# Third block's activations moved from the dense up stage to fetched rows, low parts taken on TensorE, gates spread in plain fp32

## The chip, the cores and the metric

The kernel runs on one core of a Trainium2 chip. The metric is the device time of one execution in microseconds (us), median over runs. The engines are PE (TensorE, matmuls, with its weight loads as PEld), DVE (VectorE), ACT (ScalarE), POOL (GpSimd) and SP (SyncE, which issues most DMAs). They run their own instruction streams and meet at semaphores.

## The reference

One layer of a streaming encoder over 512 tokens of width 1024 (8 chunks of 128): a mixer (stick-breaking attention and a gated short convolution), then a product-key retrieval over 16384 single-neuron experts, then a norm. The change touches the retrieval:

```
q = (x_blk @ w_q).reshape(n, PEER_HEADS, 2, PEER_HALF)        # 8 heads, two halves
s = jnp.einsum('nhpc,hpkc->nhpk', q, keys32)                  # 128 scores for each half
top_s, top_i = lax.top_k(s, PEER_TOPK)                        # first ranking: 16 of 128
cand_s = top_s[:, :, 0, :, None] + top_s[:, :, 1, None, :]    # 16 x 16 sums
best_s, best_c = lax.top_k(cand_s.reshape(...), PEER_TOPK)    # second ranking: 16 of 256
expert_idx = ...; gate = jax.nn.softmax(best_s, axis=-1)
act = jax.nn.gelu(jnp.einsum('nhkd,nd->nhk', expert_u[expert_idx], x_blk))
out = jnp.einsum('nhk,nhkd->nd', gate * act, expert_v[expert_idx])
```

So each token uses 8 x 16 = 128 experts, a row of 1024 values of `expert_u` and one of `expert_v` for each. All is fp32.

## The kernel before

Tokens are four blocks of 128. The first 487 us (the mix stage) do the mixer, the queries and the scores; it hands over the normed input `xn` transposed and split in a high part (`xnTh`, in the rounded format fp32r) and a low part (`xnTl`).

The fourth block (`SPARSE`) is done by rows: for each of its 128 slots, POOL issues an indirect DMA (`fetch`) that brings one row of 4 KB for each of 128 tokens into a ring of buffers, and DVE (`row`) forms the dot product with `x3` (rows of `expert_u`), or adds the weighted row to `acc` (rows of `expert_v`).

The first three blocks (`DB` = 3, 384 tokens) are done densely, as if every token used every expert.

**Up stage**, 128 steps, one for each group of 128 experts. In step n PE transposes the next group's `expert_u` tile into PSUM (`transposes`, 8 matmuls against the identity), ACT copies it to `uh`, rounding it (`high`), DVE subtracts to get `ul` (`low`), and PE forms activations for 384 tokens with 24 matmuls (`products`: 8 chunks times `uh`·`xnTh`, `uh`·`xnTl`, `ul`·`xnTh`). ACT applies the gelu and stores the result through its own DMA queue (`gelu`: the store of step n-2 must have landed, since `hb` has two buffers). SP loads the `u_raw` tiles four ahead.

Between the steps the gates are spread onto the 128 x 128 grid of experts. DVE ranks, finds the keys (`keys`) and builds one-hot matrices of 8 tokens (`one_hots`); ACT and POOL multiply them by the gate's high and low part (`hi`, `lo`); PE forms for 4 tokens at a time the product of one-hot and gate-one-hot, both parts side by side, 256 columns (`spread`); ACT copies them (`evac`), POOL adds the parts into `grid` (`gather`), SP stores the grid (`send`). Tables of step numbers (`HOT`, `SPREAD`, `KEYED`, `rows_of`) say in which step each engine does what; each engine works its own list in program order, and only semaphores hold it back. There is one spread in each of 96 steps.

**Down stage**, 32 turns z: 4 tiles of `expert_v` with activation times gate as weights. SP loads activations (`dh`), gates (`dg`) and values (`v_raw`); DVE multiplies (`weights`), ACT rounds (`rows_hi`, `weights_hi`), DVE subtracts (`rows_lo`, `weights_lo`) and PE does 72 matmuls of 512 columns (`down`). DVE works rows of the fourth block after the subtractions of each turn, the first 103 of its 256 rows already in the up stage. The ring has 5 buffers for the first 128 rows and 7 after. At the end the sums are added and normed.

## Time and profile before

| | us |
|---|---|
| median of 3 runs | 1715.44 (1713.63 to 1715.93) |
| span of the profiled execution | 1714.0 |
| mix stage (0 to 487) | 487 |
| up stage (487 to 1185) | 698 |
| down stage (1185 to 1707) | 522 |
| last adds and norm | 7 |

The span lies inside the range of the runs, 1.4 us under their median. The stages are cut at PE's first product, at its first matmul of the down stage and at its last matmul. PE is busy nearly all the time and runs at its full clock.

### The profile page before, as it was taken

To read this page: it belongs to the slowest core of one execution; us is meant where nothing else is said; L and a number is where in the kernel's file an instruction comes from. 1 tells how busy PE (TensorE), PEld (TensorE's weight loads), DVE (VectorE), ACT (ScalarE), POOL (GpSimd) and SP (SyncE) were. 2 spreads that over 40 slices of the span, in tenths; PEclk is the share of its full clock that TensorE was granted. 3 is DMA by queue.
4 is the path that set the end of the run, shared out by engine and by line. 5 is a ranking of instruction groups with operands and counts; after the bars stand their busy time and mean duration, and the time that the engine had idled before them with its cause. 6 is when DMAs were issued, how large, how long until landed. Compare 5 with 4: busy or idle time off the path is not lost.

```text
span 1714.0 us, 24432 instructions
## 1 busy us (share of the span) xinstructions
PE 1690.2 (99%) x9073; PEld 1510.9 (88%) x9073; DVE 1327.7 (77%) x1864; ACT 782.1 (46%) x1132; POOL 785.5 (46%) x494
## 2 busy tenths in 40 slices
PE   8999999999999999999999999999999999999998
PEld 6887788878899999999999999999888888888886
DVE  3666622265898999989999889976888888888887
ACT  6444433344333666746666566654323323323223
POOL 4333243333702555655555777771463443433430
PEclk9999999999999999999999999999999999999999
DMA  5222233322336666686667988888999999999992
GB/s 160 75 73 86 62 87 98 91 85 82 111 112 219 219 221 228 232 312 205 227 234 243 357 287 295 295 307 306 394 387 396 393 382 383 389 374 390 383 388 89
DMA packets 212443, 413.88 MB, mean 241 GB/s; under 512 B 11520, under 2 KB 150816, under 8 KB 207008
## 3 DMA queue, kind: packets, MB, share of 16 engines
q1 hardware_dynamic: 156880, 253.51, 42.4%
q0 software_dynamic: 36864, 134.23, 21.7%
q10 hardware_dynamic: 18640, 25.45, 4.2%
q8 instruction: 24, 0.39, 0.1%
q14 instruction: 35, 0.29, 0.1%
HBM read 360.73 MB, written 52.43 MB: 241 GB/s over the span
## 4 chain that ended last, share of the span: by engine, by line
PE 91%; DVE 5%; ACT 2%; issue 1%; DMA 0%; ACTq 0%; SPq 0%; DVEq 0%
PE psum L1375 30%; PE psum L1316 29%; PE psum L284 20%; PE psum L1306 6%; PE psum L1343 2%; PE psum L358 1%; PE psum L512 1%; DVE ul L1571 1%; DVE hot L1634 1%; PE psum L372 1%; PE psum L345 1%; DVE ring L1646 1%; DVE hot L1636 0%; DMA acc<-in_x 0%; ACT xTh L546 0%
## 5 line engine op out<-in xcount | busy, mean ns | idle before, releaser
L1316 PE MATMUL psum<-xnTh,uh 128*128 128x384 f32 x1024 | 353.8, 345 | 3.3 <-DVE ul L1571 3.1
L1316 PE MATMUL psum<-xnTl,uh 128*128 128x384 f32 x1024 | 343.4, 335 | 0.0
L1316 PE MATMUL psum<-xnTh,ul 128*128 128x384 f32 x1024 | 343.4, 335 | 0.0
L236 POOL TENSOR_TENSOR wl<-raw,wh 128x1024 fp32r<-128x1024 f32 x72 | 176.4, 2455 | 280.0 <-ACT wh L586 279.5
L1375 PE MATMUL psum<-vh,dwh 128*128 128x512 f32 x768 | 298.8, 389 | 0.2 <-DVE dwl L1664 0.2
L1375 PE MATMUL psum<-vh,dwl 128*128 128x512 f32 x768 | 298.8, 389 | 0.0
L1375 PE MATMUL psum<-vl,dwh 128*128 128x512 f32 x768 | 298.8, 389 | 0.0
L1530 POOL DMA_INDIRECT ring<-in_expert_v,index x128 | 170.9, 1335 | 248.9 <-DVE acc L1651 207.5
L1448 ACT ACTIVATE vh<-v_raw 128x4096 fp32r<-128x4096 f32 x31 | 112.7, 3635 | 339.0 <-PE psum L1375 338.5
L1530 POOL DMA_INDIRECT ring<-in_expert_u,index x128 | 176.1, 1375 | 165.0 <-DVE ring L1646 92.3
L1646 DVE SCALAR_TENSOR_TENSOR ring<-ring,x 128x1024 f32<-128x1024 f32 x128 | 209.7, 1659 | 6.4 <-DMA ring<-in_expert_u,index 5.1
L1549 POOL TENSOR_TENSOR grid<-parts 128x512 f32<-128x512 f32 x96 | 150.0, 1563 | 122.6 <-ACT parts L1441 98.6
L1316 PEld LDWEIGHTS psum<-xnTh,uh 128*128 128x128 f32 x1024 | 192.5, 188 | 6.5 <-DVE ul L1571 6.3
L1316 PEld LDWEIGHTS psum<-xnTl,uh 128*128 128x128 f32 x1024 | 192.7, 188 | 0.0
L1316 PEld LDWEIGHTS psum<-xnTh,ul 128*128 128x128 f32 x1024 | 192.3, 188 | 0.0
L1655 DVE TENSOR_TENSOR vl<-v_raw,vh 128x4096 fp32r<-128x4096 f32 x31 | 137.2, 4425 | 60.8 <-ACT vh L1448 60.8
L1571 DVE TENSOR_TENSOR ul<-psum,uh 128x1024 fp32r<-128x1024 f32 x128 | 155.6, 1216 | 29.6 <-ACT uh L1400 29.6
L1651 DVE SCALAR_TENSOR_TENSOR acc<-ring,weight,acc 128x1024 f32<-128x1024 f32 x128 | 164.3, 1283 | 10.7
L1375 PEld LDWEIGHTS psum<-vh,dwh 128*128 128x128 f32 x768 | 144.2, 188 | 30.3 <-issue 0.5
L1375 PEld LDWEIGHTS psum<-vh,dwl 128*128 128x128 f32 x768 | 144.2, 188 | 30.0
L1375 PEld LDWEIGHTS psum<-vl,dwh 128*128 128x128 f32 x768 | 144.2, 188 | 29.8
L284 PE MATMUL psum<-xTh,wh 128*128 128x512 f32 x424 | 168.4, 397 | 0.4 <-DVE xTl L973 0.4
(230 smaller groups left out, 2925.0 us busy)
## 6 DMA issues: line engine op xcount, KB each, us to landing
u_raw<-in_expert_u SPq DMA_DIRECT2D x128, 512.0 KB, 3.9
v_raw<-in_expert_v SPq DMA_DIRECT2D x30, 2048.0 KB, 14.6
expert_act<-hb ACTq DMA_DIRECT2D x128, 192.0 KB
expert_gate<-grid SPq DMA_DIRECT2D x12, 2048.0 KB, 7.2
dh<-expert_act SPq DMA_DIRECT2D x32, 768.0 KB, 5.6
dg<-expert_gate SPq DMA_DIRECT2D x32, 768.0 KB
raw<-in_w_in SPq DMA_DIRECT2D x40, 512.0 KB, 3.8
raw<-in_w_q SPq DMA_DIRECT2D x16, 512.0 KB, 3.9
```

What stands on the lines that cost most here:

```text
L236: nc.gpsimd.tensor_tensor(wl[slot][:], raw[slot][:], wh[slot][:].bitcast(F), ALU.subtract).then_inc(w_lo[slot], 1)
L284: done = nc.tensor.matmul(out, w[slot][:, at, :], x[:, i, :], start=(first and n == 0), stop=(last and n == 2))
L1306: last = nc.tensor.transpose(utp[s][:, c * P:(c + 1) * P], raw[n % 4][:, c * P:(c + 1) * P], ident[:])
L1316: last = nc.tensor.matmul(zb[s][:, 0:DT], w[s][:, c, :], x[:, c, 0:DT], start=(c == 0 and i == 0), stop=(c == C - 1 and i == 2))
L1375: last = nc.tensor.matmul(sums[k], w[s][:, j, b * P:(b + 1) * P], v[s][:, j, half * T:(half + 1) * T], start=(first and j == 0 and n == 0) ...
L1448: nc.scalar.activation(vh[s][:], v_raw[s][:], ACT.Copy).then_inc(v_hi[s], 1)
L1530: nc.gpsimd.indirect_dma_start(out=ring[k][:], out_offset=None, in_=tables[x // SLOTS], in_offset=bass.IndirectOffsetOnAxis(ap=index[:, x ...
L1549: nc.gpsimd.tensor_tensor(grid[:, :, n0:n0 + 4].rearrange("p k n -> p n k"), parts[x % 2][:, :, 0, :], parts[x % 2][:, :, 1, :], ALU.add). ...
L1571: nc.vector.tensor_tensor(ul[s][:].rearrange("p c f -> p (c f)"), utp[s], uh[s][:].rearrange("p c f -> p (c f)").bitcast(F), ALU.subtract) ...
L1646: nc.vector.scalar_tensor_tensor(at, at, 1.0, x3, ALU.mult, ALU.mult, accum_out=dots[:, k:k + 1]).then_inc(S["row_used"], 1)
L1651: nc.vector.scalar_tensor_tensor(acc3, at, weight[:, k:k + 1], acc3, ALU.mult, ALU.add).then_inc(S["row_used"], 1)
L1655: nc.vector.tensor_tensor(vl[s][:], v_raw[s][:], vh[s][:].bitcast(F), ALU.subtract).then_inc(v_lo[s], 1)
```

## The change

Four things are changed, and the tables of steps are written anew.

1. The third block (`MIXED`) gets its activations by fetched rows, as the fourth does: 128 more rows of `expert_u` (`x2`, `dots2`, `index2`), whose gelu then is multiplied into its gates (`gate_rows`). The dense up stage works on 256 tokens (`UT`). The down stage still has 384 columns of weights; for the third block they are the gates alone, copied from `dg`. In all 384 rows are fetched instead of 256: 203 of them are worked in the up stage, 53 by turn 9, 128 (of `expert_v`) in the 22 turns after. The ring has 7 buffers up to row 195, 5 for rows 196 to 215, then 7 others (0 to 4, 7, 8). POOL does nothing but fetch in the up stage.
2. The low part of `expert_u` tiles: PE adds minus the high part to the transposed tile in PSUM (`take_high`, 2 matmuls of 512 columns against `minus`, the negated identity, between the two halves of `products`), and ACT copies the rest as `ul` (`low`). DVE no longer takes part.
3. Gates are spread in plain fp32, 128 columns for a token: DVE builds the gate-one-hot itself with 8 small operations (`one_hots`), and ACT copies PSUM straight into one of two `grid` buffers, where neighbours lie 128 bytes apart. The first block has one spread a step (steps 40 to 71), the second and third have two (80 to 95, 104 to 119).
4. The second ranking looks at 112 of 256 sums (4 x 16 and 12 x 4), and six small operations (`cells`) turn a place among them into its two numbers.

```diff
-AHEAD = 8
...
+SEND = {spread_step(8 * q + 7) + 1: q for q in range(BATCHES // 4)}
...
+FIRST_RANKS = (11, 14, 18, 22)
+RANK_STEPS = {0: tuple(range(8, 28)), 1: (*range(37, 54, 2), 63, 65, 67)}
+KEYED = {MIXED: (4, 5, 6, 7), 0: (28, 29, 31, 33), SPARSE: (55, 57, 59, 61), 1: (69, 70, 71, 73)}
...
+GATED_IN = {5: (MIXED, SPARSE), 30: (0,), 70: (1,)}
+EXPS = {6: (MIXED, SPARSE), 31: (0,), 71: (1,)}
+GATED_OUT = {8: SPARSE, 9: MIXED, 34: 0, 74: 1}
...
+ROW_GELU, ROW_GATE = 96, 98
...
+IN_UP = 211
+LAST_DOT = 9
...
+    if n < 8 or n > 125 or n in KEY_STEP:
         return 0
...
+    if n < 28:
+        return 1 if n % 4 == 1 else 2
+    if n < 63:
+        return 1 if n % 6 == 0 else 2
+    if n < 72:
         return 0
...
+    return 3 if n % 4 == 0 else 2
...
-    return IN_UP + 5 * z if z <= 5 else SLOTS + (z - 5) * SLOTS // (2 * ROUNDS - 6)
+    if z <= LAST_DOT:
+        return FIRST_DOTS + (2 * SLOTS - FIRST_DOTS) * z // LAST_DOT
+    return min(3 * SLOTS, 2 * SLOTS + (z - LAST_DOT) * SLOTS // (2 * ROUNDS - 1 - LAST_DOT))
...
+WIDE_RING, EARLY, LATE = 196, 7, 216
...
-    for x in range(2 * SLOTS):
-        k = x % RING if x < SLOTS else (x - SLOTS) % RING_D
+    for x in range(3 * SLOTS):
+        k = x % EARLY if x < WIDE_RING else x % 5 if x < LATE else (0, 1, 2, 3, 4, 7, 8)[x % 7]
...
-    hot = [m.put(f"hot{i}", kb, [P, 8, 3, KEYS], R) for i, kb in enumerate((152, 32))]
...
+    hot = [m.put(f"hot{i}", kb, [P, 8, 2, KEYS]) for i, kb in enumerate((152, 32))]
...
-    ring = [m.put(f"ring{i}", kb, [P, D]) for i, kb in enumerate((187.75, 191.75, 195.75, 199.75, 203.75, 140, 180))]
+    ring = [m.put(f"ring{i}", kb, [P, D]) for i, kb in enumerate(
+        (187.75, 191.75, 195.75, 199.75, 203.75, 160, 164, 140, 180))]
...
             for c in range(C):
-                last = nc.tensor.transpose(utp[s][:, c * P:(c + 1) * P], raw[n % 4][:, c * P:(c + 1) * P], ident[:])
+                last = nc.tensor.matmul(utp[s][:, c * P:(c + 1) * P], raw[n % 4][:, c * P:(c + 1) * P], ident[:],
+                                        is_transpose=True, start=(c % 4 == 0), stop=True, skip_group_check=True)
...
+        def take_high(n, q=0):
...
-            pe.wait_ge(ut_lo[s], q * 2 + (n // 2 + 1))
-            pe.wait_ge(h_done[s], q * 2 + (n // 2 + PRIMED))
-            for c in range(C):
+            pe.wait_ge(ut_hi[s], q * 2 + (n // 2 + 1))
+            for half in range(2):
+                last = nc.tensor.matmul(utp[s][:, half * T:(half + 1) * T], minus[:], uh[s][:, 4 * half:4 * half + 4, :],
+                                        start=False, stop=True, skip_group_check=True)
+            last.then_inc(ut_sub[s], 1)
+        def products(n, q=0, chunks=range(C)):
...
-                    last = nc.tensor.matmul(zb[s][:, 0:DT], w[s][:, c, :], x[:, c, 0:DT],
+                    last = nc.tensor.matmul(zb[s][:, 0:UT], w[s][:, c, :], x[:, c, 0:UT],
...
         def step(n, q=0):
             transposes(n + 1, q)
-            products(n, q)
+            products(n, q, range(0, C // 2))
+            take_high(n + 1, q)
+            products(n, q, range(C // 2, C))
...
             for n in range(4):
                 at = 4 * half + n
-                last = nc.tensor.matmul(gp[:, n * 2 * P:(n + 1) * 2 * P], hot[s][:, at, 0, :],
-                                        hot[s][:, at, 1:3, :].rearrange("p g k -> p (g k)"), start=True, stop=True)
+                last = nc.tensor.matmul(gp[half][:, n * P:(n + 1) * P], hot[s][:, at, 0, :], hot[s][:, at, 1, :],
+                                        start=True, stop=True)
...
-                step(n, q)
+                step(n0 + n, q)
+                if EVERY[b] == 2:
+                    spread(k0 + n // 2, n % 2, q)
+                else:
+                    for half in range(2):
+                        spread(k0 + n, half, 2 * q)
...
+        def low(n):
+            s, r = n % 2, n // 2
+            act.wait_ge(ut_sub[s], r + 1)
+            if n == 0:
+                act.wait_ge(w_made[1], tiles + PRIMED)
+            nc.scalar.activation(ul[s][:].rearrange("p c f -> p (c f)"), utp[s], ACT.Copy).then_inc(ut_lo[s], 1)
...
-            nc.scalar.activation(hb[s][:], zb[s][:, 0:DT], ACT.Gelu).then_inc(h_done[s], 1)
+            nc.scalar.activation(hb[s][:], zb[s][:, 0:UT], ACT.Gelu).then_inc(h_done[s], 1)
...
-        def hi(k):
...
-                last = nc.scalar.activation(hot[s][:, n, 1, :], hot[s][:, n, 2, :].bitcast(F), ACT.Copy,
-                                            scale=gate_hi[:, t:t + 1].bitcast(F))
...
+            nc.scalar.activation(grid[q % 2][:, :, n0:n0 + 4].rearrange("p k n -> p n k"),
+                                 gp[half].rearrange("p (n k) -> p n k", n=4), ACT.Copy).then_inc(S["g_evac"], 1)
...
+            act.wait_ge(dg_in[s], r * 16 + 16)
+            nc.scalar.activation(wh[s][:, :, UT:DT].rearrange("p j (b n) -> p j b n", n=32),
+                                 dg[s][:, UT // 32:DT // 32, :, :].rearrange("p b j n -> p j b n"), ACT.Copy)
...
-                hi(HOT[n])
+                low(n + 1)
```

On PE, in a step of the second block's spreads (`uh`, `ul` the tile's parts, `u_raw` the tile to be transposed, `hot` the one-hots). Before:

```order
L1306 MATMUL psum<-ident,u_raw_66 128x128 x8
L1316 MATMUL psum<-xnTh,uh_123 128x384
L1316 MATMUL psum<-xnTl,uh_123 128x384
L1316 MATMUL psum<-xnTh,ul_125 128x384
...
L1343 MATMUL psum<-hot_131 128x256 x4
```

Now:

```order
L1336 MATMUL psum<-ident,u_raw_68 128x128 x8
...
L1357 MATMUL psum<-xnTh,uh_123 128x256
L1357 MATMUL psum<-xnTl,uh_123 128x256
L1357 MATMUL psum<-xnTh,ul_125 128x256
L1345 MATMUL psum<-uh_124,minus 128x512 x2
...
L1386 MATMUL psum<-hot_131 128x128 x4
...
L1386 MATMUL psum<-hot_131 128x128 x4
```

The products are narrower, two matmuls that wait for ACT's `uh` of the next tile stand in their middle, and there are two groups of spreads.

On ACT in the same place (`hb` the activations, `parts` or `grid` the spread gates). Before:

```order
L1407 ACTIVATE hb_127<-psum 128x384 [waits h_out1,u_mm1]
L1409 DMA expert_act<-hb_127 128x384 [waits h_done1]
L1441 ACTIVATE parts_130<-psum 128x1024 [waits g_sum,g_full0]
L1400 ACTIVATE uh_123<-psum 128x1024 [waits u_mm1,ut_full1]
L1431 ACTIVATE hot_131<-hot_131,gate_hi 128x128 [waits hot_eq]
L1431 ACTIVATE hot_131<-hot_131,gate_hi 128x128 x7
```

Now:

```order
L1475 ACTIVATE hb_128<-psum 128x256 [waits h_out1,u_mm1]
L1477 DMA expert_act<-hb_128 128x256 [waits h_done1]
L1501 ACTIVATE grid_129<-psum 128x4x128 [waits g_full1] x2
L1460 ACTIVATE uh_124<-psum 128x1024 [waits u_mm1,ut_full1]
L1468 ACTIVATE ul_126<-psum 128x1024 [waits ut_sub1]
```

The tile's low part is ACT's, the eight scaled one-hots are gone.

On POOL, where the ring changes. Before, at row 128:

```order
L1530 DMA ring_147<-in_expert_v,index 128x1024 [waits row_used]
L1530 DMA ring_148<-in_expert_v,index 128x1024 [waits row_used]
L1530 DMA ring_149<-in_expert_v,index 128x1024 [waits ut_full1]
L1530 DMA ring_150<-in_expert_v,index 128x1024
L1530 DMA ring_144<-in_expert_v,index 128x1024 [waits row_used]
```

Now, at rows 214 to 218 (`ring_150` is buffer 0):

```order
L1602 DMA ring_154<-in_expert_u,index_144 128x1024 [waits row_used]
L1602 DMA ring_150<-in_expert_u,index_144 128x1024 [waits row_used]
L1602 DMA ring_158<-in_expert_u,index_144 128x1024 [waits hot_ready1]
L1602 DMA ring_150<-in_expert_u,index_144 128x1024 [waits row_used]
L1602 DMA ring_151<-in_expert_u,index_144 128x1024 [waits row_used]
```

Buffer 0 is asked for row 217 two rows after row 215, and what follows on POOL waits behind it.

## Rows read from the trace of the kernel before

**Rows 1.** The page: busy time; the chain's shares by line.

```profile
PE 1690.2 (99%) x9073; PEld 1510.9 (88%) x9073; DVE 1327.7 (77%) x1864; ACT 782.1 (46%) x1132; POOL 785.5 (46%) x494
...
PE psum L1375 30%; PE psum L1316 29%; PE psum L284 20%; PE psum L1306 6%; PE psum L1343 2%; PE psum L358 1%; PE psum L512 1%; DVE ul L1571 1%; DVE hot L1634 1%; PE psum L372 1%; PE psum L345 1%; DVE ring L1646 1%; DVE hot L1636 0%; DMA acc<-in_x 0%; ACT xTh L546 0%
```

**Rows 2.** Windows by stage: us, busy of each engine (instructions), PE's clock, DMA share, GB/s.

```profile
487.00:1185.00 698.00, 695.31 (x4473) 691.01 (x4473) 622.88 (x976) 406.55 (x751) 391.37 (x252) 1.00 0.74 256
1185.00:1707.00 522.00, 521.85 (x2302) 432.30 (x2303) 441.94 (x295) 162.38 (x81) 200.37 (x148) 1.00 0.96 363
```

**Rows 3.** Chain in order of time (start, us, what): a plain step of the up stage.

```profile
511.60 0.87 PE psum L1306 x8
512.47 4.17 PE psum L1316 x24
```

**Rows 4.** The same, a step with a spread.

```profile
697.34 4.19 PE psum L1316 x24
701.52 0.47 PE psum L1343 x4
```

**Rows 5.** The same, end of the mix stage: plain fp32, 512 columns, ranking.

```profile
469.88 0.89 PE psum L512 x8
470.77 5.46 PE psum L284 x24
...
478.27 0.89 DVE top L1030 x4
```

**Rows 6.** Timeline, all engines (start, us, what): step 7, then a table load after step 8.

```profile
526.59 1.03 PE L1306 MATMUL psum<-ident,u_raw 128*128 128x128 f32 x8
526.79 0.49 ACT L1407 ACTIVATE hb<-psum 128x384 f32<-128x384 f32 x1 [3.08 <-PE psum L1316]
...
527.75 1.03 ACT L1400 ACTIVATE uh<-psum 128x1024 fp32r<-128x1024 f32 x1 [0.47 <-PE psum L1306]
...
532.73 1.28 ACT L1412 ACT_TABLE_LOAD   x1 [0.40 <-ACT hb L1407]
```

**Rows 7.** Timeline of ACT near the end of the up stage.

```profile
1150.28 0.34 ACTq L1409 DMA_DIRECT2D expert_act<-hb  x1
...
1160.05 0.49 ACT L1407 ACTIVATE hb<-psum 128x384 f32<-128x384 f32 x1 [3.26 <-DMA expert_act<-hb]
```

**Rows 8.** Timeline of POOL, then of DVE, at the same moment.

```profile
703.63 2.24 POOL L1549 TENSOR_TENSOR grid<-parts 128x512 f32<-128x512 f32 x1 [2.43 <-ACT parts L1441]
...
704.61 2.33 DVE L1646 SCALAR_TENSOR_TENSOR ring<-ring,x 128x1024 f32<-128x1024 f32 x1
```

**Rows 9.** The line of the dot products (ns: min/median/max).

```profile
L1646 DVE SCALAR_TENSOR_TENSOR ring<-ring,x x128: 1206/1221/4126, 548.5 to 1265.0; 128x1024 f32<-128x1024 f32 x128
```

**Rows 10.** Groups by line: busy us, mean ns | idle before.

```profile
L1646 DVE SCALAR_TENSOR_TENSOR ring<-ring,x 128x1024 f32<-128x1024 f32 x128 | 209.7, 1659 | 6.4 <-DMA ring<-in_expert_u,index 5.1 <-ACT selT L1422 1.3
...
L1651 DVE SCALAR_TENSOR_TENSOR acc<-ring,weight,acc 128x1024 f32<-128x1024 f32 x128 | 164.3, 1283 | 10.7
L1571 DVE TENSOR_TENSOR ul<-psum,uh 128x1024 fp32r<-128x1024 f32 x128 | 155.6, 1216 | 29.6 <-ACT uh L1400 29.6
```

**Rows 11.** Timeline of DVE in the down stage, one turn.

```profile
1521.54 6.83 DVE L1651 SCALAR_TENSOR_TENSOR acc<-ring,weight,acc 128x1024 f32<-128x1024 f32 x5
1528.29 1.75 DVE L1671 TENSOR_TENSOR dh<-dh,dg 128x1536 f32<-128x1536 f32 x1
1531.85 4.43 DVE L1655 TENSOR_TENSOR vl<-v_raw,vh 128x4096 fp32r<-128x4096 f32 x1 [1.81 <-ACT vh L1448]
```

**Rows 12.** Windows inside the down stage, columns as in rows 2.

```profile
1190.00:1670.00 480.00, 480.00 (x2119) 397.59 (x2118) 410.77 (x260) 146.40 (x60) 196.30 (x146) 1.00 1.03 387
1200.00:1360.00 160.00, 160.00 (x707) 132.55 (x706) 134.28 (x101) 50.39 (x21) 70.85 (x51) 1.00 1.04 393
```

**Rows 13.** DMA issues in the down stage: count, KB each, us to landing.

```profile
v_raw<-in_expert_v SPq DMA_DIRECT2D x29, 2048.0 KB, 14.6
...
ring<-in_expert_v,index POOLq DMA_INDIRECT x126, 11.8
```

511 lines of the change are left out of this document (258 added, 253 removed).

## The prediction

> **What bounds the kernel now.** I read the page first: PE is busy 1690.2 of 1714.0 us, and the chain of waits goes through PE's lines almost alone, 30% down stage (L1375), 29% products (L1316), 20% mix [rows 1]. The windows by stage say the same of each part: PE 695.3 of 698 us in the up stage and 521.9 of 522 in the down stage, clock 1.00, the other engines well below [rows 2]. So a matmul taken from PE is worth its own time, as long as nothing else becomes late: DVE (622.9 of 698) is next, then DMA (256 GB/s in the up stage, 363 in the down stage).
>
> A step's make-up is in the chain: 0.87 for 8 transposes, 4.17 for 24 products [rows 3], 0.47 more for a spread [rows 4]. 128 × 5.04 + 96 × 0.47 = 690.2, and the stage has 698: some 8 us are waits and edges.
>
> **PE's own work.**
> - A product of 384 columns costs 4.17/24 = 0.1738 us, a spread matmul of 256 columns 0.47/4 = 0.1175 [rows 3, 4]. 128 × 24 = 3072 products go from one to the other: −172.9 us.
> - Two `take_high` matmuls of 512 columns a step: 5.46/24 = 0.2275 each [rows 5], × 256 = +58.2.
> - A spread is now four plain fp32 matmuls of 128 columns. Eight records of such work take 0.89 [rows 5], the same sum as two passes for each of four. 96 × (0.89 − 0.47) = +40.3.
> - Sum −74.4. A plain step becomes 0.87 + 2.82 + 0.455 = 4.15 us, with one spread 5.04, with two 5.93.
>
> The down stage keeps its 72 matmuls a turn, and the mix stage is unchanged. The gain stands in the up stage: 690.2 − 74.4 = 616 us of PE work.
>
> **What comes back there.** A shorter step leaves less time for what lay beside it.
>
> *ACT's table loads.* A load is 1.28 us [rows 6], and each of three softmaxes needs two, with exps between: a stop of some 3.3 us. Before, `uh` was wanted a whole step later; now `take_high` wants it at the middle of the step. I take 2.5 us for each of the three stops against about half before: +6, between 0 and +10.
>
> *The round trip in mid-step.* ACT began the rounding 1.16 us after the first transpose began (527.75 against 526.59), and took 1.03 [rows 6], so `uh` is there at +2.19, some 0.05 more for the semaphore. PE is through its first 12 products at 0.87 + 12 × 0.1175 = +2.28. That fits by 0.05 us. ACT's stages (`hb`, now about 0.4, `uh` 1.03, `ul` 1.03, a grid copy of about 0.6 for 512 elements going by `hb` and `uh`) fill 2.5 to 3.7 of 4.15 to 5.93 us. I take +4 for single misses, between 0 and 32 (0.25 a step).
>
> *The store of the activations.* The gelu of step n waits until the store of n−2 has landed. That store is issued about 0.5 us after its gelu began, so two steps cannot be shorter than its latency L plus 0.5. In two steps of 5.04 there was room for L = 9.6; two of 4.15 leave 7.8. Near the end of the old stage one store issued at 1150.28 was still waited for at 1160.05, L = 9.7, and ACT stood 3.26 us for it [rows 7]. How often will that be? The stage moved 256 GB/s × 698 = 179 MB [rows 2]. It now fetches 100 more rows of 0.524 MB, stores 8.4 MB less: 223 MB in some 645 us, 345 GB/s. By the tables of steps, the second half (from step 72, 2.25 rows a step) asks for 400 to 440 GB/s, and the best 160 us of the down stage moved 393 [rows 12]. So transfers queue there. A plain step held back by L = 9.7 costs 0.95 us; there are 64 plain steps, 32 before step 40 and about 30 after 72. I take fifteen of them, +14, for store and traffic together. The ends are 0 (step 7's kind of landing throughout) and +40.
>
> *DVE.* From 622.9 go 155.6 for the subtractions [rows 10]. The dot products took 209.7 us for 128 [rows 10] though their median is 1.221 [rows 9]: the long ones, as 2.33 us, stood beside POOL's additions of 2.24 [rows 8], which leave, so about −53. Added are 100 rows × 1.3 = +130 and 48 × (8 × 0.22 − 1.2) = +26, 0.22 being a ranking operation of that width (0.89 for four) [rows 5]. About 570 of 645 us: DVE stays beside PE. I give it nothing; a wait on DVE would show as PE's wait for `hot`.
>
> *Edges.* The first weighted products of the down stage need ACT's high and low parts after the last gelu: +4 (0 to 8). Of the 8 us of waits and edges of before, half go with the subtraction they waited for: −4.
>
> **The down stage.** A turn is 522/32 = 16.3 us.
>
> *DVE.* Before, a turn had 6.83 for 5 rows, 1.75 and 4.43 for weights and subtraction [rows 11], and a second subtraction. Now 5.8 rows of 1.28 [rows 10] are 7.5, and its weights are a third fewer, 1.2: 7.5 + 1.2 + 4.43 + 1.9 = 15.0 of 16.3. It fits by 1.3 us.
>
> *DMA.* Before, values, activations and gates were 3.67 MB a turn and 5 rows 2.62: 6.29 MB in 16.3 us, 385 GB/s, as the window has it (387) [rows 12]. Now 3.41 + 5.84 × 0.524 = 6.47 MB, 396 GB/s. The best stretch had 393 [rows 12]. Two to three GB/s too much over 500 us is 0.7%, less what the prefetch absorbs: +2 (0 to 10).
>
> *Rows at the change of rings.* Rows 196 to 215 have 5 buffers, with 6 rows a turn, and row 217 waits for row 215's buffer. A row lands 11.8 us after its issue [rows 13], and so the rows of turns 3 and 4 come late; DVE stands in front of a row, and behind it stand the subtractions that PE waits for: +6 (0 to 12).
>
> The second ranking over 112 cells only shortens DVE's part, off the path: 0. Start of the stage and tail: +1.
>
> **Sum.** −74.4 + 6 + 4 + 14 + 4 − 4 + 2 + 6 + 1 = −41.4. From the profiled span 1714.0 that is 1672.6; the median stands 1.4 above the span, so **1674 us**.
>
> **A rule against the change.** The window shows 387 GB/s moved for 480 us without a break, at a share of 1.03 [rows 12], so a core can draw that much. The Trainium skill, in "DMA: Bandwidth & Descriptors", section "Where 436 GB/s comes from", puts the limit between HBM and SBUF at about 358 GB/s for a core. By that rule the down stage's 204 MB would want 570 us, 48 more than it has, and the forecast would be 1722; the stage of before already ran above that figure, so the trace disagrees, and I go by the trace.
>
> **The rivals.**
> 1. *The mid-step round trip misses in every step.* If `uh` comes 0.3 us late, 128 × 0.25 = +32, less the store waits that vanish in longer steps (−10): about 1696. For it: a margin of 0.05. Against: the measured +2.19.
> 2. *The grid copies are slow.* They write elements 128 bytes apart, and no row of before shows ACT doing that; bounds are 0.49 us for the 384 of `hb` [rows 6], and 2.24 for POOL's 512 written into the same grid [rows 8]. At some 1.3 us two of them push `uh` back by 0.95 in the 32 two-spread steps and one by 0.55 in the other 32: +48, less 10: about 1712, which would be no change. The Trainium skill, "SBUF — State Buffer", in the section "Door 1: The DMA port swizzle (why `[64,N]` ≈ `[32,N]`)", speaks for this: it says of 16-byte lines that each access crossing to a new one pays; it gives no time, and the rival's price is from the rows above.
> 3. *DMA or DVE takes over the down stage.* If the traffic holds at 387 GB/s, a turn of 6.47 MB takes 16.7 us, +0.4 × 32 = 13, with later rows at the ring change about +20 in all: 1694.
> 4. *The activations' stores bind the up stage; slower.* If traffic near 390 GB/s gives them the latency of a ring row, 11.8 us [rows 13], each plain step becomes (11.8 + 0.5)/2 = 6.15 and each one-spread step too: 64 × 2.0 + 32 × 1.1 = +163 in place of +14, far above 1800. It turns to slower than before from a mean L of about 9.5, which holds the 64 plain steps at 5.0: +54 in place of +14. With L = 10 on the mean (steps of 5.25) it is 64 × 1.1 + 32 × 0.21 = +77, about 1737. For it: one store of 9.7 us at lower traffic [rows 7]. Against: in step 7 ACT waited only for PE [rows 6], and slower steps ask for less traffic, which shortens L.
> 5. *Nothing comes back but ACT's table loads and edges*: 1655.
>
> **How the numbers follow.** Chances: forecast (1658 to 1690) 0.55, rival 1 0.12, rival 2 0.08, rival 3 0.10, rival 4 0.07, rival 5 0.08. The range has to leave out no more than 2 in 10: it takes in the forecast, rivals 1, 3 and 5, and stops short of 2 and 4 (0.15): 1652 to 1708. A measurement can tell 0.2% (3.4 us) from no change. Faster: everything but rival 4 and half of rival 2, 0.88; same 0.04; slower 0.08.
>
> **What the changed profile would show.** The stages: up about 645 us, down about 530. Product groups of 12 at 1.41 us, `take_high` pairs at 0.455, spreads at 0.89. The idle time before `take_high` and what ended it (ACT's `uh`) measures rival 1, the mean of ACT's grid copy rival 2 (0.6 against 1.3). ACT's `hb` with a wait for a DMA landing, summed over the stage, measures the store term, 14 us against above 40. In the down stage PE's 72 matmuls a turn and GB/s (above or below 393) tell rival 3, and DVE's wait for a `ring` landing in turns 2 to 5 the ring term. The dot products should all be near 1.22 us with POOL only fetching. I am wrong at the root if PE's products are not 0.1175 each at clock 1.00, and wrong in the returns if the up stage stands above 665 or under 625 us.

## The result, and the profile after

The changed kernel takes **1690.59 us** (median of 4 runs, 1686.95 to 1696.12), the kernel before 1715.32 beside it: a ratio of 0.986 (95% interval 0.9837 to 0.9882), 24.7 us faster. The forecast was 1674 us, with a range of 1652 to 1708. Run once more on another occasion it took 1688.73 us (1686.12 to 1690.97; 0.9842, interval 0.9825 to 0.9858). The profiled execution has a span of 1694.4 us, so it is the slowest of the four, some 5 us above the median; the sum of the forecast stood at a span of 1672.6.

The page's busy time [rows 1], and then the windows by stage [rows 2], columns as there:

```profile
PE 1634.6 (96%) x9712; PEld 1442.6 (85%) x9712; DVE 1244.9 (73%) x2365; ACT 792.6 (47%) x909; POOL 721.8 (43%) x478
```

And the windows:

```profile
485.70:1143.30 657.60, 633.79 (x5121) 620.30 (x5119) 537.89 (x1386) 418.36 (x498) 279.35 (x208) 0.99 0.89 337
1143.30:1683.20 539.90, 529.25 (x2304) 435.47 (x2304) 456.38 (x374) 161.03 (x106) 253.79 (x176) 0.99 0.97 364
1683.20:1694.40 11.20, 0.00 (x0) 0.00 (x0) 6.26 (x15) 3.77 (x11) 0.00 (x0) 0.61 0.36 140
```

PE lost 55.6 us of work but its share fell from 99% to 96%: it now waits. The mix stage takes 485.7 us (before 487), the up stage 657.6 (before 698, forecast about 645), the down stage 539.9 (before 522, forecast about 530), what follows PE's last matmul 11.2 (before 7). So 40 us were won in the up stage, and 18 + 4 given back behind it.

PE's own work came out within 2% of its sum. The chain in order of time in a plain step [rows 3] and in one with two groups of spreads [rows 4]:

```profile
502.56 0.87 PE psum L1336 x8
503.43 1.43 PE psum L1357 x12
504.86 0.46 PE psum L1345 x2
505.32 1.42 PE psum L1357 x12
...
871.09 1.79 PE psum L1386 x16
```

0.87 + 1.43 + 0.46 + 1.42 = 4.18 (forecast 4.15), 1.79 for 16 records of spreads (2 x 0.89). From the starts of PE's matmuls a plain step takes 4.19 us, one with one group of spreads 5.11 and one with two 6.03 to 6.05; 112 of 127 steps are within 0.12 us of that pattern. What the others have more is this, in the profiled run:

| steps | more than the pattern, us | what stands there |
|---|---|---|
| 7, 8 / 32, 33 / 72 | 4.8 / 4.5 / 4.4 | ACT's two table loads |
| 51 / 75 / 99, 100 / 123 | 1.1 / 1.2 / 4.9 / 2.1 | ACT waits for a store of activations |
| 125 | 1.8 | first rounding of values, 1.9 us on ACT |
| 126, 127 | 8.1 | second rounding of values (PE idle 1.4); then PE idle 6.2 for the first weights of the down stage |
| all steps | some 9 | 0.04 to 0.12 a step over the forecast's 4.15, 5.04 and 5.93; 0.33 at each of three transposes of gates (also before) |

PE's waits have the first two lines of the table as waits for ACT's `uh`, and the end, with the down stage, as waits for DVE's weights (us, times, longest):

```profile
PE psum L1345 <- ACT uh L1460: 17.6, 9, 3.0
PE psum L1433 <- DVE dwl L1727: 16.8, 6, 7.4
```

**The table loads.** The chain behind step 6 (rows 6 show such a load before the change), and the windows around it (PE's clock is the number between POOL's and the DMA share):

```profile
515.15 0.39 ACT hb L1475
...
515.94 0.14 ACT L1480
516.07 1.16 issue
517.23 0.69 ACT sel L1484 x2
...
517.94 1.28 ACT L1485
...
519.24 1.03 ACT uh L1460
...
520.31 0.73 PE psum L1345 x2
521.04 1.89 PE psum L1357 x12
522.93 1.71 PE psum L1336 x8
```

The windows there:

```profile
515.00:520.00 5.00, 2.42 (x21) 2.21 (x19) 2.70 (x13) 4.41 (x6) 3.78 (x5) 1.00 0.67 228
520.00:524.00 4.00, 3.69 (x20) 3.61 (x21) 1.81 (x6) 1.67 (x3) 3.39 (x3) 0.72 1.02 409
...
528.00:532.00 4.00, 4.00 (x35) 3.91 (x34) 3.97 (x17) 2.36 (x3) 2.34 (x2) 1.00 1.02 410
```

`uh`, wanted 2.3 us into the step, is there after 5.4. Behind the stop of 3 us the 12 products take 1.89 and the transposes 1.71 us, in place of 1.43 and 0.87: the granted clock is 0.72 of 2.4 GHz on the mean of 4 us, a part of them at 1.2. So here the stop costs 3.1 us and the clock 1.7 more. The drop does not follow every such stop: in the trace of e_ring, an edit of a later stage (below), PE stands as long at this place and the clock stays full:

```profile
521.00:525.00 4.00, 4.00 (x34) 3.91 (x34) 1.97 (x8) 2.44 (x3) 3.09 (x4) 1.00 1.02 410
```

**A store of activations.** The chain ahead of steps 99 and 51 [rows 7]:

```profile
968.14 11.35 DMA expert_act<-hb
...
708.36 10.87 DMA expert_act<-hb
...
719.25 0.02 ACTq L1474
...
719.31 0.39 ACT hb L1475
```

The grids' stores of 2 MB are issued in twelve steps. Behind ten of them (48, 72, 84 to 96, 108 to 120) a store of activations took 9.1 to 11.4 us, where the median of all 128 is 5.7; the steps with two groups of spreads are long enough to hide that, and only behind the stores of steps 48, 72, 96 and 120 did PE stop.

**The end of the up stage.** The chain through it:

```profile
1100.27 13.52 DMA expert_gate<-grid
...
1113.87 23.98 DMA dg<-expert_gate
...
1137.94 1.23 DVE dh L1734
```

The last grid is stored (13.5 us), then the gates of the first turn are loaded (24.0), and DVE starts the first weights at 1137.94, when PE's last product has ended (1137.0); PE then stands for 6.2 us.

**The down stage.** PE's turns of 72 matmuls are 16.32 us as before, but the fourth takes 23.9 and the fifth 18.2. In the chain of waits, a row of the ring lands 12 and then 10 us after its issue while DVE stands before it:

```profile
1172.61 11.97 DMA ring<-in_expert_u,index
...
1198.82 10.27 DMA ring<-in_expert_u,index
```

The DMA issues of the stage [rows 13]:

```profile
v_raw<-in_expert_v SPq DMA_DIRECT2D x29, 2048.0 KB, 21.9
...
ring<-in_expert_v,index POOLq DMA_INDIRECT x128, 8.4
```

Values land after 21.9 us at the median (before 14.6). A part of that is SP's: its issue of the values, behind that of the gates, takes 6.2 us at the median and up to 12.0, before the change 1.0 and up to 8.4:

```profile
1316.57 9.26 SPq L1261 DMA_DIRECT2D v_raw<-in_expert_v  x1
```

From turn 19 on ACT gets some of the values late, and PE loses 6 us in ten turns.

### The profile page after: what moved, and what is told of

Same layout as the page of the kernel before. It is cut to its first block, busy times and chain, and to the rows that moved or that the text cites. A ratio compares the mean times of both kernels' runs of the same rounds, so it can differ in the third digit from the quotient of the medians.

```text
span 1694.4 us, 25882 instructions
## 1 busy us (share of the span) xinstructions
PE 1634.6 (96%) x9712; PEld 1442.6 (85%) x9712; DVE 1244.9 (73%) x2365; ACT 792.6 (47%) x909; POOL 721.8 (43%) x478
## 4 chain that ended last, share of the span: by engine, by line
PE 59%; DMA 22%; DVE 8%; ACT 6%; issue 4%; SPq 1%; POOL 1%; ACTq 0%; DVEq 0%
PE psum L286 21%; PE psum L1357 19%; DMA v_raw<-in_expert_v 16%; PE psum L1336 6%; PE psum L1386 5%; PE psum L1345 3%; ACT vh L1509 3%; DVE vl L1715 2%; DMA expert_act<-hb 2%; DMA ring<-in_expert_u,index 2%; DMA dg<-expert_gate 1%; DVE dwl L1727 1%; PE psum L1433 1%; PE psum L360 1%; PE psum L514 1%
## 5 line engine op out<-in xcount | busy, mean ns | idle before, releaser
L1602 POOL DMA_INDIRECT ring<-in_expert_u,index x256 | 357.4, 1396 | 462.1 <-DVE ring L1706 374.7
L1706 DVE SCALAR_TENSOR_TENSOR ring<-ring,x 128x1024 f32<-128x1024 f32 x256 | 303.1, 1220 | 67.2 <-DMA ring<-in_expert_u,index 67.0
L1357 PE MATMUL psum<-xnTh,uh 128*128 128x256 f32 x1024 | 300.9, 294 | 0.0
L1357 PE MATMUL psum<-xnTh,ul 128*128 128x256 f32 x1024 | 290.3, 284 | 0.0
L1357 PE MATMUL psum<-xnTl,uh 128*128 128x256 f32 x1024 | 290.2, 283 | 0.0
L1602 POOL DMA_INDIRECT ring<-in_expert_v,index x128 | 175.7, 1373 | 189.9 <-DVE acc L1711 155.3
L1357 PEld LDWEIGHTS psum<-xnTl,uh 128*128 128x128 f32 x1024 | 196.4, 192 | 5.6
L1357 PEld LDWEIGHTS psum<-xnTh,ul 128*128 128x128 f32 x1024 | 196.0, 191 | 0.0
L1468 ACT ACTIVATE ul<-psum 128x1024 fp32r<-128x1024 f32 x128 | 131.4, 1027 | 111.0 <-PE psum L1345 107.8
L286 PE MATMUL psum<-xTh,wl 128*128 128x512 f32 x424 | 165.4, 390 | 0.0
```

The lines of the kernel that those rows point to most:

```text
L286: done = nc.tensor.matmul(out, w[slot][:, at, :], x[:, i, :], start=(first and n == 0), stop=(last and n == 2))
L1357: last = nc.tensor.matmul(zb[s][:, 0:UT], w[s][:, c, :], x[:, c, 0:UT], start=(c == 0 and i == 0), stop=(c == C - 1 and i == 2))
L1468: nc.scalar.activation(ul[s][:].rearrange("p c f -> p (c f)"), utp[s], ACT.Copy).then_inc(ut_lo[s], 1)
L1602: nc.gpsimd.indirect_dma_start(out=ring[k][:], out_offset=None, in_=tables[x // SLOTS], in_offset=bass.IndirectOffsetOnAxis(ap=numbers[x / ...
L1706: nc.vector.scalar_tensor_tensor(at, at, 1.0, of, ALU.mult, ALU.mult, accum_out=dots[:, k:k + 1]).then_inc(S["row_used"], 1)
```

## The experiments

All are edits of the changed kernel; the changed kernel's two sets of runs (1690.6, 1688.7) are what they are held against.

**The same kernel again.** (after_again) No edit.

> The changed kernel as it is, once more, so that the three variants run beside it on one chip. Its four runs spread over 9 us (1686.95 to 1696.12), those of the kernel before over 2.3. If the spread comes from DMA landings (stops of PE behind ACT's wait for a store, at steps 51, 75, 99, 123, 125 of the profiled run), this one's profile has such stops at other steps and a sum for them that differs by several us; the three stops at the table loads (steps 7, 32, 72; 2.8 us each) stand at the same steps with the same length. If the spread comes from elsewhere, the same steps show the same excess. Time: 1685 to 1697.

Measured: 1688.73 us (1686.12 to 1690.97). Table loads at the same steps with 4.8, 4.5 and 4.2 us; the other stops again at 51, 75, 99 and 123, with 1.4, 0.8, 3.0 and 2.2 us, and 7.6 at the end. So the stops have fixed places, which I had not expected, and their lengths vary.

**Four buffers for the activations.** (e_hb4)

```
-    hb = [... for i in range(2)]
+    hb = [... for i in range(4)]
-    act.wait_ge(h_out[s], r * 16 + PRIMED * 16)
+    if n >= 4:
+        act.wait_ge(h_out[n % 4], n // 4 * 16)
```

Two small tiles of the ranking were moved to make room.

> Four buffers for the activations in place of two, so that the gelu of step n waits for the store of n-4. Theory (the two-buffer wait costs PE its stops outside the table loads): no ACT hb wait for a DMA landing is left, steps 51, 75, 99, 123, 125 and their like are 4.19 or 5.11 us as their neighbours, up stage some 11 us shorter than the 657.6 of the changed kernel, median about 1680. Rival (the stores are late because DMA is saturated, and then something else that waits for DMA, a u_raw tile or a row, takes the stop over): under 3 us gained, and PE's or DVE's waits for u_raw or ring landings grow by what ACT's shrink.

Measured: 1690.65 us (1686.89 to 1699.1; 0.9875), no gain. The profiled execution is the fastest of its four, so its trace flatters it by some 4 us. The stops at 51, 75, 99 and 123 are gone (7 us in the repeated run), but PE now waits 3.6 us in step 104 for one-hots and loses 1.6 more to the clock, and the stage's end has 8.2 us as before. PE's waits (the first is mostly the down stage's fourth turn):

```profile
PE psum L1434 <- DVE dwl L1729: 14.9, 4, 8.0
PE psum L1346 <- ACT uh L1461: 11.3, 5, 2.9
...
PE psum L1387 <- DVE hot L1696: 3.6, 1, 3.6
```

The chain ahead of step 104 has rows of the ring that land after 17.8 and 16.3 us, with DVE's one-hots behind them:

```profile
981.38 16.27 DMA ring<-in_expert_u,index
```

The mechanism of the theory is right and its worth wrong: the rival's words hold, something else that waits for DMA takes the stop over.

**Seven buffers from row 203.** (e_ring)

```
-WIDE_RING, EARLY, LATE = 196, 7, 216
+WIDE_RING, EARLY, LATE = 196, 7, 203
```

> The down stage's seven buffers are used from row 203 on in place of row 216; nothing else changes. Theory (five buffers between two turns' subtractions make the rows of turns 2 to 4 late): PE's stop of 7.4 us at the fourth turn and the slower clock behind it (1.9) go, DVE's waits for ring landings in the down stage fall from 36.8 to under 15 us, median 6 to 9 us less, about 1683. Rival (DMA is full at 390 GB/s there, and more buffers only queue more rows): the stop stays within 3 us of its length, or moves to ACT's wait for v_raw; median within 3 us of the changed kernel's.

Measured: 1676.64 us (1674.88 to 1677.7; 0.9777, interval 0.976 to 0.9793), 12 to 14 us less. The turns are 16.32 us from the second on but for 1 us in two late ones, and the runs differ by 3 us where they differed by 9. PE's waits (above for the changed kernel):

```profile
PE psum L1345 <- ACT uh L1460: 17.4, 9, 2.9
...
PE psum L1433 <- DVE dwl L1727: 4.0, 2, 3.4
```

The rival (DMA full, more buffers only queue more) falls: the stage moved its rows in time. DVE's wait for ring landings in the down stage falls from 21.0 us to 2.6. The down stage is 525.1 us, 13.1 less than in the repeated run and 14.8 less than in the first; stop and clock of the fourth and fifth turn are 9.5 to 10 of that, the late turns 2 to 5.5. Its up stage was also 3.5 us shorter than the repeated run's, with no edit there, and 3 of these stand at the table loads: behind two of the three stops the clock stayed full (10.4 us more than the pattern in place of 13.5). That part is chance.

**Third block's gates four steps earlier.** (e_gates)

```
-TURN = (36, 76, 100)
+TURN = (36, 76, 96)
-ROW_GELU, ROW_GATE = 96, 98
+ROW_GELU, ROW_GATE = 93, 95
```

> The third block's gates are spread in steps 100 to 115 in place of 104 to 119 (its scores' gelu in step 93, its gates in 95), so the last grid is stored some 17 us earlier. Theory (PE starts the down stage late because the first gates are loaded only after the last grid's store, 13.5 us, and then take 24 us to land): the gap of some 8 us ahead of PE's first matmul of the down stage goes, and with it the slow clock of the first 3 us; median 8 to 10 us less, about 1682. Rival (rows and tiles fill DMA there, and ACT's and DVE's first parts are as late by v_raw's landing or by rows): the gap stays above 4 us, released by another line; median within 4 us of the changed kernel's.

Measured: 1690.98 us (1686.1 to 1694.62; 0.9857), nothing. The grid was stored earlier, but in SP's order the gates' load stands behind the last tiles of `expert_u`, and so it was issued at 1111.69 in place of 1113.87, and took 25.8 us:

```profile
1110.76 0.33 SPq L1258
...
1111.69 25.80 DMA dg<-expert_gate
```

**Exponentials between the two copies.** (e_explate)

```
                 high(n + 1)
+                if n - 1 in EXPS:
+                    exps(*EXPS[n - 1])
                 low(n + 1)
             gelu(n)
-            if n in EXPS:
-                exps(*EXPS[n])
```

> ACT does the exponentials and the two table loads of steps 6, 31 and 71 one step later and between the rounding of the next tile and the copy of its low part, in place of ahead of the rounding. Nothing else changes. In the changed kernel each of these stops PE for 2.8 us (take_high stands at 5.1 to 5.4 us of its step, not 2.30), and 1.7 us more go in the slower clock that follows. The low part is wanted about 2.1 us later in the step than the high part, so the stop should fall to 1.5 to 2 us. Theory (a stop of 2 us or less leaves the clock alone, as at steps 123 and 125, one of 2.8 does not): 1 us of stop and 1.7 of clock go three times, up stage 7 to 8 us shorter, median about 1682. Rival (the clock falls after any stop in a table load): 3 us, 1687. Second rival (spans of 1686 to 1696 come from other causes and hide it): the three steps' sum tells, which is 15 us in the changed kernel.

Measured: 1682.64 us (1678.25 to 1686.93; 0.9811, interval 0.9787 to 0.9835), 6 to 8 us less. The three places have 1.9, 1.6 and 1.7 us more than the pattern (13.7 before), and the clock stays full behind all three; behind the first:

```profile
518.00:522.00 4.00, 2.73 (x22) 2.31 (x20) 2.49 (x6) 3.52 (x4) 3.08 (x4) 1.00 1.01 404
522.00:526.00 4.00, 3.93 (x32) 3.83 (x32) 3.90 (x18) 2.29 (x4) 2.08 (x3) 1.00 1.02 404
```

The time is what the theory forecast, and the three shorter stops left the clock alone. Its rule, that a stop of 2 us or less does so and one of 2.8 does not, is not borne out by the traces taken together (last section).

**No table loads** (e_noexp; the exponential left out, a plain copy in its place).

```
-            nc.scalar.preload_act_table_set("exp_and_others")
...
-                nc.scalar.activation(gates, gates, ACT.Exp, ...)
+                nc.scalar.activation(gates, gates, ACT.Copy, ...)
-            nc.scalar.preload_act_table_set("gelu_and_others")
```

> Leaves work out: the gates' exponential is a plain copy and no table is loaded, so the gates are not softmax values; all else runs as in the changed kernel. It measures what the three table changes cost altogether. Theory: stops of 2.8 us and 1.7 us of slower clock behind each, 13 to 15 us for three, so the three places (steps 7, 32, 72) are 4.19 us long and the median is about 1676. Rival (only the stop counts, the clock falls anyway): 8 us, 1682. If the time goes down by less than 4 us the stops were made good later by something that ends the up stage in any case, the load of the first gates.

Measured: 1680.21 us (1679.37 to 1686.38; 0.9792), 9 to 10 us less, between theory and rival. The three places are down to 0.5, 0 and 0.6 us. In the profiled execution, the slowest of the four and 6 us above the median, the stops for stores at 75, 76 and 99, 100 are 5.3 and 6.0 us (1.2 and 4.9 in the changed kernel); how much of that the median run has is not known. The store ahead of step 75:

```profile
823.62 11.66 DMA expert_act<-hb
```

**Low parts on DVE again.** (e_lowdve)

```
             transposes(n + 1, q)
-            products(n, q, range(0, C // 2))
-            take_high(n + 1, q)
-            products(n, q, range(C // 2, C))
+            products(n, q)
...
-                low(n + 1)
...
+            if n:
+                low(n)
```

The last two lines stand in DVE's program, where `low` subtracts as it did before the change; the line taken out above them is ACT's.

> Undoes the second part of the change alone: the low parts of the tiles are DVE's subtraction again, at the head of DVE's step, and PE's take_high and ACT's copy are gone (from the second tile on). PE's work falls by 127 x 0.46 = 58 us, DVE's grows by 127 x 1.22 = 155. Theory (DVE could not carry it): DVE was busy for 538 of the 658 us of the up stage and 105 of 120 between 1000 and 1120 us; with 693 it binds, PE waits in most steps with rows or one-hots for ul, and the up stage is 700 to 740 us, the median 1730 to 1770. Rival (DVE's rows are taken up in the slack of other steps, and PE's gain shows): up stage 620 to 650, median 1655 to 1685. It also shows whether PE's stops at the table loads go with the mid-step wait: they should be under 1 us each, as before the change.

Measured: 1934.51 us (1929.41 to 1937.01; 1.128), far slower than either forecast: an up stage of 902 us. And not for want of DVE's time, which was busy for 72% of the span. PE's and DVE's waits:

```profile
PE psum L1357 <- DVE ul L1736: 253.7, 90, 7.1
```

DVE's:

```profile
DVE hot L1687 <- PE psum L1384: 186.7, 30, 7.0
```

PE waits 254 us for `ul`, and DVE 187 us for PE to be done with the one-hots of the step before, each behind the other in one order. I had added up busy times (693 us); the wait in a ring of two engines is what counted. A part of it is the clock: it was granted at 0.88 on the mean of the stage, where PE stands so often. So the second part of the change is worth 244 us with these tables of steps; what it would be worth with tables made for the other way was not tried.

**Grids stored in four pieces.** (e_split)

```
-            load(r, range(2))
-            if 4 * r - 4 in SEND:
-                send(SEND[4 * r - 4])
-            load(r, range(2, 4))
+            for s in range(4):
+                if s >= 2 and 4 * r - 4 in SEND:
+                    send(SEND[4 * r - 4], s - 2)      # the second argument: which quarter
+                if s < 2 and 4 * r - 8 in SEND:
+                    send(SEND[4 * r - 8], s + 2)
+                load(r, (s,))
```

> SP stores each grid of 2 MB in four pieces of 0.5 MB, one between two u_raw loads each, where it stored it in one piece. Nothing else changes. In the changed kernel the stops of PE outside the table loads stand at steps 51, 75, 99 and 123, each three steps behind a grid's store (steps 48, 72, 96, 120), and the activations' store issued just before took 9 to 11 us there, 1.7 to 7 elsewhere. Theory (the big store fills the queues for 6 us and the small one stands behind it): those four stops fall from 7 to 10 us together to under 3, and the median is 5 to 8 us lower, about 1682. Rival (the stores are late because DMA moves all it can, 410 GB/s, whatever its pieces): stops of the same sum at other steps, median within 3 us of 1690; the last grid also lands no earlier, and the first gates come late as before.

Measured: 1685.96 us (1684.81 to 1689.9; 0.9834, interval 0.9818 to 0.9851), 3 to 5 us less at the median; its interval overlaps that of the repeated run, so the gain is not shown. The stops at 51, 75, 99 and 123 are gone, as the theory has it; smaller ones stand at 93, 104, 113 and 117 (5.0 us), and at step 125 ACT waits 6.9 us for the last grid's last piece:

```profile
1124.42 1.91 ACT L1522 ACTIVATE vh<-v_raw 128x2048 fp32r<-128x2048 f32 x1 [6.90 <-DMA expert_gate<-grid]
```

Of the stores of activations whose landing the trace has (64 of 128) the slowest took 8.1 us, 11.4 in the changed kernel. So the 2 MB store in one piece is what the activations' store was late behind; the time goes elsewhere, and the up stage is 654.9 us as in the repeated run (654.8). The first gates' load, issued last here, took 8.1 us.

**Contiguous grid copies** (e_flat; the numbers stand in the wrong places of the grid; as many are moved).

```
-            nc.scalar.activation(grid[q % 2][:, :, n0:n0 + 4].rearrange("p k n -> p n k"),
-                                 gp[half].rearrange("p (n k) -> p n k", n=4), ACT.Copy)
+            nc.scalar.activation(grid[q % 2][:].rearrange("p k n -> p (k n)")[:, n0 * KEYS:(n0 + 4) * KEYS], gp[half], ACT.Copy)
```

> Leaves something out: ACT writes each group of gates contiguously (128 x 512 as they stand in PSUM), not 128 bytes apart, so the stored grids have their numbers in the wrong places; as many bytes are moved. It measures the strided copy, which took 1.10 us in the changed kernel where 0.6 was forecast. Theory (the stride costs ACT about 0.5 us a copy and nothing of PE's, since the next rounding began in time): the copy takes 0.55 to 0.62 us, PE's steps with two groups stay at 6.00 to 6.07 us, median within 3 us of 1690. Rival (the late copy holds back the spreads): these 32 steps shorten to 5.95 and the 32 with one group from 5.11 to 5.07, 4 us in all, median 1686.

Measured: 1686.3 us (1685.27 to 1688.44; 0.9828, interval 0.9812 to 0.9845), which does not set it apart from the repeated run. The groups by line, changed kernel and this one:

```profile
L1501 ACT ACTIVATE grid<-psum 128x512 f32<-128x512 f32 x96 | 100.8, 1117 | 32.0 <-PE psum L1386 31.6 <-ACT hb L1475 0.4
```

And without the stride:

```profile
L1501 ACT ACTIVATE grid<-psum 128x512 f32<-128x512 f32 x96 | 57.3, 597 | 41.5 <-PE psum L1386 41.1 <-ACT hb L1475 0.4
```

The stride costs 520 ns of 1117. PE's steps with two groups go from 6.05 us at the median to 5.98, those with one from 5.11 to 5.09: about 3 us for all 64.

**Five edits together, three ways.** (e_best1, e_best2, e_best3) e_ring, e_hb4, e_gates and e_explate in one, and in the first also SP's load of the first gates ahead of the last two tiles:

```
+        def first_gates():
+            for out_ in g_out:
+                sp_.wait_ge(out_, (STORES + PRIMED) * 16)
+            load_gates(0, slice(0, 1))
...
             load(r, range(2))
+            if r == STEPS // 4 - 1:
+                first_gates()
...
-        for out_ in g_out:
-            sp_.wait_ge(out_, (STORES + PRIMED) * 16)
-        load_gates(0, slice(0, 1))
```

> Five edits together: seven buffers from row 203 (as e_ring, 1676.6), four activation buffers (as e_hb4), third block's gates four steps earlier (as e_gates), exponentials between the two copies (as e_explate), and SP loads the first gates ahead of the last two u tiles, where it loaded them after them. Alone, hb4 and gates gave nothing. Theory (they gave nothing because the last wait of the up stage, the load of the first gates, 22 to 26 us long and issued at 1110 to 1114 us in all of them, ended it in any case): with that load issued some 8 to 10 us earlier, stores, table loads and gates all count, PE's gap ahead of the down stage falls from 8 us to under 3, and the median is 1650 to 1660. Rival (DMA is full from step 80 on, and whatever is moved comes late elsewhere): 1670 or more, with new waits for ring landings, u_raw or hot in steps 104 to 127.

Measured: **1666.78 us** (1664.09 to 1670.06; 0.9719, interval 0.9702 to 0.9736). That is 24 us under the changed kernel and 49 under the one before, and lies between theory and rival. The ring and the exponentials alone gave 12 to 14 and 6 to 8 us, so the other three edits added little. PE does the down stage without a stop, its wait ahead of it is 1.5 us; but the `u_raw` tile issued behind the gates takes 26 us, and PE stands 10.7 us for it in step 124:

```profile
1089.71 26.46 DMA u_raw<-in_expert_u
```

and PE's waits:

```profile
PE psum L1340 <- DMA u_raw<-in_expert_u: 10.7, 1, 10.7
```

In the second, ACT issues that load at step 120 from its own queue, and SP does not:

```
+            if n == STEPS - 8:
+                for out_ in g_out:
+                    act.wait_ge(out_, (STORES + PRIMED) * 16)
+                act.dma_start(dg[0][:].rearrange("p b j n -> p b (j n)"),
+                              gv[:, :, 0:1, :].rearrange("p b o x -> p b (o x)")).then_inc(dg_in[0], 16)
```

> As e_best1, but ACT issues the load of the first gates at step 120 from its own queue, so that no u_raw tile stands behind it; SP waits for nothing there. Theory (the stop of 10.7 us for a u_raw tile at step 124 was made by SP waiting for the grid's store ahead of the last two tile loads): that stop goes, gates land by 1125 us, PE begins the down stage within 3 us after its last product, and the median is 9 to 12 us below e_best1's 1666.8, about 1656. Rival (on ACT's queue the gelu's stores stand behind the gates' 1536 packets of 512 bytes, and the last gelus wait for their buffers): a stop of several us at steps 124 to 127 with ACT hb waiting for a DMA landing, median 1662 to 1667.

Measured: **1665.84 us** (1664.25 to 1670.76; 0.9708, interval 0.9692 to 0.9724), the same, and in the rival's range, though neither at its steps nor by its wait: ACT does not wait for a store's landing, the issue of the next store itself takes ACT 8.43 us in place of 0.34, and the rounding behind it is late.

```profile
1089.49 0.45 ACTq L1537 DMA_DIRECT2D dg<-expert_gate  x1
1090.04 1.03 ACT L1457 ACTIVATE uh<-psum 128x1024 fp32r<-128x1024 f32 x1 [1.02 <-PE psum L1333]
...
1093.74 8.43 ACTq L1475 DMA_DIRECT2D expert_act<-hb  x1
1102.27 1.02 ACT L1457 ACTIVATE uh<-psum 128x1024 fp32r<-128x1024 f32 x1 [8.57 <-issue]
```

In the third, the load is in two pieces, two thirds of it at step 104, and the first rounding of values in four:

```
+            if r == 27:
+                for q in range(2):
+                    sp_.wait_ge(g_out[q], (2 * UT // 64 // 2 + PRIMED) * 16)
+                first_gates(slice(0, UT // 32))
...
-        load_gates(0, slice(0, 1))
+        first_gates(slice(UT // 32, DT // 32))
```

> As e_best1, with the first gates loaded in two pieces: the first two blocks' (1024 packets of 512 bytes) at step 104, as soon as their grids are stored, the third block's (512 packets) after the last u_raw tiles; and with the first rounding of values cut in four pieces of one tile, in steps 122 to 125, where two pieces of two tiles stood in steps 124 and 125. Theory (the first gates' load, 22 to 26 us wherever it stood, ended the up stage: as a wait of its own at the end, as a u_raw tile's 26 us behind it in e_best1, as a full ACT queue in e_best2): a third of it left for the end lands in about 10 us, no stop of 8 to 11 us is left between steps 120 and 127, the excess of steps 125 and 126 (5 us) falls by half, and the median is 1652 to 1658. Rival (those packets cost the same wherever they are, since DMA is full from step 80 on): the stop moves to step 104 to 110, behind a u_raw tile or a row, and the median stays at 1663 to 1668.

Measured: 1674.65 us (1673.63 to 1676.18; 0.9764), worse than both. The stage's end now has a stop of 9.0 us all the same, and the gates are not in its chain any more; rows of the ring are, up to 20.7 us in landing:

```profile
1085.39 20.66 DMA ring<-in_expert_u,index
...
1107.57 12.28 DMA ring<-in_expert_u,index
```

And step 8 has 8.8 us more than the pattern, where e_best1 has 1.9: PE, ACT and SP stand still from 524 us on for some 3.5 us with no semaphore to wait for by the trace, while the first rows come in. No other variant has this. What it is stays open.

## Why the prediction was right, and where its sizes were off

The sign, the range and the mechanism hold: PE's work fell by what the sum says, the gain came in the up stage, and part of it was given back by the named mechanisms. The size was 25 of the 41 us. By the steps of the sum, in the profiled run (span 1694.4 against 1672.6; a median run has some 5 less):

- **PE's work**, forecast 4.15, 5.04 and 5.93 us a step: 4.19, 5.11 and 6.05 by the starts of matmuls, at the median. Right; the 0.04 to 0.12 are some 9 us in all, of which e_flat explains 3.
- **Table loads**, forecast +6: 13.7 us. This is the step that was mis-sized most. The +6 is three stops of 2.5 us less half a microsecond each for what was there before, and that much was right: the kernel before has PE idle for 0.65, 0.34 and 0.34 us there. The stops are 2.7 to 3.1 us, and the clock behind them, in no term of the sum, took 1.7 more each time in this run (but behind one of three only in e_ring's).
- **Mid-step round trip** (rival 1), +4 forecast: 0. `take_high` begins 2.30 us into the step in all undisturbed ones. The margin of 0.05 us held.
- **Stores of activations**, +14 forecast: 9.3, 1.7 of it the clock behind step 99. Right mechanism, and not the place: not fifteen plain steps at random, but the third step behind four of the twelve grids' stores (e_split), and when the stops are taken away the time comes back elsewhere (e_hb4, e_split). The working also had the plain steps wrong: of the 64, 40 stand before step 40 and 24 after step 72, not 32 and about 30. The stage moved 337 GB/s, 345 forecast.
- **Rival 2**, slow grid copies at 1.3 us: they are 1.12, near the rival, but it did not happen: `take_high` begins on time in all undisturbed steps with spreads too, so the copy's place in ACT's step had room. Only in step 51, where a late store had held ACT, does the copy stand in the chain ahead of the rounding, from 720.11 to 721.00. The page named beside it ("SBUF — State Buffer", section "Door 1: The DMA port swizzle (why `[64,N]` ≈ `[32,N]`)", of the Trainium skill) said that such an access pays: it does, 1117 against 597 ns.
- **Edges of the up stage**, +4 forecast: 9.9 (1.8 in step 125, 8.1 at the end). Some 3 of that are the two roundings of values, and 6.2 the load of the first gates, which the sum left out: a queue of SP that I did not follow to its end.
- **DVE beside PE**, about 570 us forecast: 538. Right. The products are at 1.22 us throughout with POOL only fetching, as the rows 8 and 9 let expect.
- **Change of rings**, +6 forecast: 9.5 with the slower clock, and e_ring gains 12 to 14. Right mechanism and place, the fourth turn, 3.5 us too small.
- **DMA in the down stage**, +2: 6.4 in the profiled run, in ten turns from the 19th on, where values land late; 0.1 in those of e_gates and e_explate, with the same down stage, and 1.0 in e_ring's. So it differs from run to run, and 2 was its order. At 1340 to 1500 us the stage moved 380 to 403 GB/s; the sum had 396. Rival 3 did not happen: e_ring holds 16.32 us a turn. The Trainium skill's 358 GB/s ("DMA: Bandwidth & Descriptors", "Where 436 GB/s comes from") did not bind after the change either: e_ring moved 377 GB/s on the mean of its down stage of 525 us.
- **Start and tail**, +1 forecast: 1.6 for the clock in the first turn, 4.9 at the end (11.3 us behind the end of PE's last matmul, 6.4 before). The chain there goes through DVE's last rows and adds, and not through PE. That the extra row a turn is the cause is likely and not shown; no run was made on this.
- **Rival 4**, stores that bind: a share of it is there (latencies of 9 to 11 us did occur), at no time for a stretch of steps; the median store took 5.7 us.
- **Rival 5** stands at 1655, but the terms that it keeps (table loads, edges, start) come to some 1648, below the range's lower end. It plays no part in the result.

DMA as what binds the end of the up stage was in the prediction as one sentence (400 to 440 GB/s asked from step 72 on), and its worth as part of +14. The experiments point to it as the limit of that stage's last third: six edits that take a wait away there (e_hb4, e_gates, e_split and the three last) each show another transfer late in its place, at 388 GB/s on the mean from 1000 to 1140 us. That is argued and not shown, since no edit asked for less traffic there. Whether fewer rows in steps 96 to 125 would win it back was not tried.

## What to carry to other kernels

Cost a shorter step twice: once by the work taken out, and once by every wait that used to hide in it, with the latency and the deadline side by side. Where a wait is taken away on a full DMA, look for the transfer that is next late before counting the gain; only the edits that let transfers start earlier (the ring) or that ask for none (the table loads) kept most of it. Two engines that wait for each other within a step cannot be costed by adding busy times.

## What the runs showed of the hardware

- The clock behind a stop of PE, by the twelve traces of the changed kernel and its edits without e_lowdve: of 28 stops of 2.2 to 3.1 us, 23 were followed by 1.2 GHz for a while, some 1.7 us lost each time, and 5 were not (2.90 and 2.59 us in e_ring, 2.90 in e_split, 2.69 in the repeated run, 2.61 in e_flat). Of six stops of 1.8 to 2.0 us three were (1.78 in e_flat, 1.96 in e_gates, 1.93 in the changed kernel's down stage); of 47 stops of 0.9 to 1.7 us none was. So the length of a stop alone does not decide it; what does, these runs do not show.
- An ACT copy from PSUM of 128 x 512 fp32 takes 597 ns into contiguous SBUF, and 1117 ns where neighbours lie 128 bytes apart.
- A load of 768 KB in packets of 512 bytes, the first gates, took 18.7 us (e_ring) to 27.7 us (e_best1), and 8.1 us in e_split, where it was issued last. Behind it on the same queue, a DMA issue took its engine 8.43 us in place of 0.34 on ACT (e_best2) and 8.79 in place of 0.33 on SP (e_best1), where the tile of 512 KB then landed after 26.5 us in place of 6.6. In the down stage SP's issue of 2 MB behind each such load took 6.2 us at the median.
- Beside a store of 2 MB issued shortly before on SP's queue, a store of 128 KB on ACT's took 9.1 to 11.4 us, against a median of 5.7; with the large one in four pieces (e_split) the slowest of the 64 whose landing the trace has took 8.1.
